# Weight splits on GpSimd cut into four pieces of 256 columns in most slots of a hybrid decoder step

## The chip, the cores and the metric

The kernel runs on one core of a Trainium2 chip. The metric is the time of one execution on the device in microseconds (us); the kernel before has a median of 2016.64 us over 3 runs (2014.04 to 2017.82).

## What is computed

One step of a one-layer decoder for two request groups that share all weights: a prompt of 1024 tokens and 8 samples of 4 tokens, together 1056 columns. The model width is 1024, everything is float32. Cut to what matters here:

```python
xn = rmsnorm(x, p["norm_mix_g"])
aq, ak, av, dq, dk, dvv, dz, da, db, ga, gb = split_cols(xn @ p["w_in"], IN_SPLITS)
ya = swa_prompt(aq, ak, av, p["sinks"])                     # window attention (sample: with cache)
qkv, new_dn_buf = causal_dwconv(jnp.concatenate([dq, dk, dvv], axis=-1), dn_buf, p["dn_conv_w"])
dq, dk, dvv = jnp.split(jax.nn.silu(qkv), 3, axis=-1)
o, new_S = gated_delta(qh, kh, heads(dvv), g, beta, dn_state, chunk)
yb = (rmsnorm(o, p["dn_norm_g"]) * jax.nn.silu(heads(dz))).reshape(B, L, DN_WIDTH)
mix = jax.nn.sigmoid(ga) * (ya @ p["w_br_a"]) + jax.nn.sigmoid(gb) * (yb @ p["w_br_b"])
h = x + mix @ p["w_mix_out"]
mk, mv = jnp.split(rmsnorm(mem, g) @ w_xkv, 2, axis=-1)     # memory keys and values
h = h + cross_attention(rmsnorm(h, p["norm_x_g"]) @ p["w_xq"], mk, mv) @ p["w_xo"]
u, gv = jnp.split(rmsnorm(h, p["norm_ffn_g"]) @ p["w_up"], 2, axis=-1)
u, new_ffn_buf = causal_dwconv(u, ffn_buf, p["ffn_conv_w"])
h = h + (jax.nn.silu(u) * gv) @ p["w_down"]
y = rmsnorm(h, final_norm_g)
```

The step also returns the new caches and states. It is one launch for both groups.

## The kernel before, in words

**A product in three.** A float32 matrix product is made of three products of numbers that are cut to fewer bits: weight W is split in a high part WH (W written in the type fp32r, with less of its mantissa) and a low part WL = W - WH, the activations x in XH and XL in the same way, and TensorE sums WH·XH + WH·XL + WL·XH into PSUM (`gemm_part`, line L542; `down`, L1969, has AH and AL in the place of XH and XL; `end_down`, L2001, has LASTH and LASTL; `gate_parts`, L1360). The 1056 columns go through in three chunks of 352. So one weight slot, of 128 rows by 1024 columns, is 8 blocks of 128 x 128 by 3 products by 3 chunks: 72 matmuls.

**Slots.** All weights lie in 136 slots of 512 KB, used in one order: attention 0 to 5, gate_a 6 to 9, the delta rule's q, k, v (dn) 10 to 21, gate_m 22 and 23, gate_b 24 to 29, dz 30 to 33, gate 34 to 37, branch 38 to 45, mix_kv 46 to 61, xq 62 to 65, xo 66 to 69, and the feed-forward stage 70 to 135, four in iteration 0 and six in each of iterations 1 to 10 (four for the up products of iteration f, then two for the `down` product of iteration f - 1; slots 132 and 133 are `down` of iteration 9). The last two, 134 and 135, are for `end_down`, which does the last `down` chunk by chunk with the final norm behind it. gate_m, gate_b and gate stand for tiles of the branch gates' product; those of slots 6 to 9 and 22 to 29 are early ones, stored in DRAM and loaded back later. In the delta stage, after the convolution of slots 22 and 23, `gate_parts` feeds small portions of these gate products into the gaps of the delta rule's chunks.

**Three engines per slot.** Slot n uses buffer p = n % 2 of RAW, WH and WL.
- SyncE's `loads` brings slot n's weights into RAW[p] once slot n-2 has been split (semaphore w_split). Its other transfers (gates, states, outputs) stand in the same queue.
- GpSimd's `split` waits for raw_in[p] (weights landed) and for w_used to reach n-1 (slots 0 to n-2 are used up, so the buffer is free). It writes WH = RAW * 1 (L755), adds 1 to w_hi, waits for w_hi, writes WL = RAW - WH (L757) and adds 1 to w_split. Its `one` is a constant of one column, broadcast over the free axis. Slot n is thus split while TensorE works on slot n-1.
- TensorE waits for w_split to reach n+1, runs the slot's matmuls, and adds 1 to w_used.

Slots 46 to 63 (HALVES) are split in two halves of 512 columns by `split_half` (L769 high, L771 low), the first half with semaphores of its own, so that a half can be split as soon as half a slot is used. All other slots are split whole, in two instructions. GpSimd has no other work, but for 19 adds of squares (L789, L792) for the final norm, which are behind the last split in its program.

**VectorE and ScalarE.** VectorE makes the low parts of the activations (L522 in `plain_rest`, L2452 in `split_rests`, L2617 in `rests`), the residual adds (L2597 in `mlp_down`), and the elementwise work between products. The places that the prediction goes through:
- Convolution of the delta rule's q, k, v (L2183 to L2209), with ScalarE's Silu (L929) behind it; small preparations of the next stage (L2401).
- Delta stage. `front` (L2273 to L2297) prepares a chunk of 128 tokens: t1, t2, t3 (L2276, L2278, L2280) make the decay masks, then a, q, k (L2284 to L2291) and v; `invert_quarters` (L2342 to L2361) inverts the chunk's triangular matrix by levels, alternating with TensorE (L1558): L2348 and L2355 are VectorE's steps, and each waits for TensorE's product before it and is waited for by the next one. `state` (L2371, L2373) multiplies the state by the decay and adds the chunk's update. All of this is one program order on VectorE.
- z multiply (L2447), after the delta stage.
- Branch products (L2459, L2463, L2465): for each tile t of 8, the gate times the accumulated product for both branches, and their sum. After t = 3 stand the seven adds of squares of the memory's norm (`norm_add`, L465), after t = 5 its eight scalings (`norm_dve`, L509) and eight low parts (L503), of 256 columns each; slot 45 is split during this.
- First norm of the feed-forward stage: L522 and L465 for eight tiles, then TensorE sums over partitions with a matrix of ones (`norm_sum`, L478).
- The last iteration of the feed-forward stage: `rests` (the two subtractions L2617) is put before `mlp_down` of the iteration before, and not behind it as in the others. While these run, TensorE begins slot 132 and GpSimd splits slot 133; TensorE's `down` waits for fd_free, which the residual adds L2597 raise. VectorE's line:

```python
if last:
    rests()
if not (isinstance(f, int) and f == 0):
    mlp_down(f - 1, FFN0(f) + 4)
if not last:
    rests()
```

**GpSimd's program order** around the change: `pairs(pool, 46, split)` (a loop over pairs of slots), the unrolled halves of 46 to 63, then a loop over pairs for 64 to 135, then the adds of squares.

Of the kernel before, what the change touches and what calls it, by code (L numbers as in the profile page):

```python
# [15 lines left out]
F32 = mybir.dt.float32  # L16
F32R = mybir.dt.float32r
ALU = mybir.AluOpType
# [21 lines left out]
SLOT = KT * P  # L40


SLOTS = {}
# [31 lines left out]


HALVES = SLOTS["mix_kv"][0], SLOTS["xq"][0] + 2
TURN = KT // 2
LEVEL_PARTS = (0, 3, 6, 8, 11, 14, 16, 20)
UNIT0 = 3 * (GA + GM)  # L80
# [60 lines left out]
def build(nc, d):  # L141
    ctx = ExitStack()
    with ctx:
        def sb(name, shape, dt=F32):
            return ctx.enter_context(nc.sbuf_tensor(name, shape, dt))

        def sem(name):
            return ctx.enter_context(nc.semaphore(name))

        def wait(eng, s, v):  # L150

            if not (isinstance(v, int) and v <= 0):
                eng.wait_ge(s, v)

        def pairs(eng, n, body):

            body(0, 0)
            body(1, 1)
            if n > 2:
                with eng.Fori(1, n // 2) as i:  # L160
                    body(2 * i, 0)
                    body(2 * i + 1, 1)
# [11 lines left out]
        RAW = sb("RAW", [P, 2, SLOT])  # L174
        WH = sb("WH", [P, 2, SLOT], F32R)
        WL = sb("WL", [P, 2, SLOT], F32R)
# [10 lines left out]
        def cst(name):  # L187
            a, n = CONST[name]
            return CST[:, a:a + n]
# [186 lines left out]
        def end_direct(c, m):  # L376

            return c == NCH - 1 and m >= KT - 2

        def end_add(c, m):  # L380
            return len([1 for x in END_UNITS[:END_UNITS.index((c, m)) + 1] if x[1] > 0 and not end_direct(*x)])
# [40 lines left out]
        raw_in = [sem("raw_in0"), sem("raw_in1")]  # L422
        w_hi, w_split, w_used = sem("w_hi"), sem("w_split"), sem("w_used")
# [17 lines left out]
        n = 0  # L441
# [5 lines left out]
        def norm_square(act, i, k, src, w):  # L447

            sq, ss, rs = norm_space(i)
            if k < 2:  # L450
                wait(act, nlo, 8 * i)
            else:
                act.wait_ge(nadd, 7 * i + max(1, k - 2))
            nc.scalar.activation(sq[:, k % 2, 0:w], src[:, k, :], ACT.Square).then_inc(nsq, 1)
# [60 lines left out]
        def plain_head(i, k, b, gain):  # L515

            nc.scalar.activation(XH[:, b, :], H[:, k, :], ACT.Copy, scale=gain[:, k:k + 1]).then_inc(nhi, 1)
# [8 lines left out]
        def gemm_tile(mm_g, p, k0, kn, off, xk0=0, ready=None, turn=0, between=None):  # L526

            for k in range(kn):
                if ready is not None:
                    nc.tensor.wait_ge(ready[0], ready[1] + xk0 + k + 1)  # L530
                mm = gemm_part(mm_g, p, k, kn, off, (k + turn) % KT - k if turn else xk0)
                if between is not None and k == between[1]:
                    between[0]()
            return mm
# [213 lines left out]
        @block.gpsimd  # L748
        def _(pool):
            one = cst("ones")[:, 0:1].to_broadcast([P, SLOT])  # L750

            def split(n, p, more=0):
                pool.wait_ge(raw_in[p], 8 * (n - p) + 16)
                wait(pool, w_used, n - 1)
                nc.gpsimd.tensor_tensor(WH[:, p, :], RAW[:, p, :], one, ALU.mult).then_inc(w_hi, 1)  # L755
                pool.wait_ge(w_hi, n + 1 + more)
                nc.gpsimd.tensor_tensor(WL[:, p, :], RAW[:, p, :], WH[:, p, :].bitcast(F32),  # L757
                                        ALU.subtract).then_inc(w_split, 1)
            pool.wait_ge(const_in, 16)
            def split_half(n, h):  # L760

                p, half = n % 2, slice(SLOT // 2 * h, SLOT // 2 * h + SLOT // 2)
                if h == 0:
                    pool.wait_ge(raw_in[p], 8 * (n - p) + 16)
                if h == 0 and n >= HALVES[0] + 2:
                    pool.wait_ge(w_half, n - HALVES[0] - 1)
                else:
                    pool.wait_ge(w_used, n - 1)
                nc.gpsimd.tensor_tensor(WH[:, p, half], RAW[:, p, half], one[:, 0:SLOT // 2], ALU.mult).then_inc(w_hi, 1)  # L769
                pool.wait_ge(w_hi, HALVES[0] + 2 * (n - HALVES[0]) + h + 1)  # L770
                nc.gpsimd.tensor_tensor(WL[:, p, half], RAW[:, p, half], WH[:, p, half].bitcast(F32),  # L771
                                        ALU.subtract).then_inc(w_split if h else w_first, 1)

            def rest_split(n, p):
                split(n, p, HALVES[1] - HALVES[0])
            pairs(pool, HALVES[0], split)
            for n in range(*HALVES):
                split_half(n, 0)
                split_half(n, 1)
            with pool.Fori(HALVES[1] // 2, NSLOTS // 2) as i:  # L780
                rest_split(2 * i, 0)
                rest_split(2 * i + 1, 1)

            for u, (c, m) in enumerate(END_UNITS):
                if m == 0 or end_direct(c, m):
                    continue
                pool.wait_ge(e_sqr, u + 1)
                if m == 1:
                    nc.gpsimd.tensor_tensor(e_ss[:, c, :], e_sq[:, (u - 1) % 6, :], e_sq[:, u % 6, :], ALU.add).then_inc(e_add, 1)  # L789
                else:  # L790
                    pool.wait_ge(e_add, end_add(c, m - 1))
                    nc.gpsimd.tensor_tensor(e_ss[:, c, :], e_ss[:, c, :], e_sq[:, u % 6, :], ALU.add).then_inc(e_add, 1)  # L792
# [3 lines left out]
        def _(act):  # L796
# [436 lines left out]
            for k in range(KT):  # L1233
                if k == KT - 1:
                    act.wait_ge(w_used, SLOTS["xo"][0] + 4)
                    for t in range(TURN, KT - 1):
                        plain_head(3, t, (t + TURN) % KT, cst("g_ffn"))
                act.wait_ge(xo_free, k + 1)
                if k < TURN or k == KT - 1:
                    plain_head(3, k, (k + TURN) % KT, cst("g_ffn"))  # L1240
                norm_square(act, 3, k, H, T)
# [51 lines left out]
        def _(pe):  # L1293
# [716 lines left out]
            def mlp_pe(f):  # L2010
                first = isinstance(f, int) and f == 0
                for j in range(4):
# [9 lines left out]
                    if first and j == 0:  # L2022
                        pe.wait_ge(xo_free, 7)
                    gemm_tile(j % 2, j % 2, 0, KT, 0, ready=(nlo, 24) if first and j == 0 else None, turn=TURN,
                              between=(lambda: norm_sum(pe, 3), KT - 2) if first and j == 0 else None).then_inc(w_used, 1)
# [9 lines left out]
        def _(dve):  # L2035
# [506 lines left out]
            for t in range(8):  # L2542
# [5 lines left out]
                if 2 <= t < 7:  # L2548
                    norm_add(dve, 3, t - 1, T)
                if 1 <= t <= TURN:  # L2550
                    plain_rest(dve, 3, t - 1, t - 1 + TURN, cst("g_ffn"))
# [209 lines left out]
```

## Time and profile before

| | before |
|---|---|
| runs, median (lowest to highest) | 2016.64 us (2014.04 to 2017.82) |
| profiled execution, own time | 2019.54 us |
| profiled execution, span of the trace | 2017.8 us |
| TensorE busy with matmuls | 1901.5 us, 94% |
| TensorE busy loading weights (beside matmuls) | 1789.3 us, 89% |
| VectorE busy | 1004.3 us, 50% |
| ScalarE busy | 489.3 us, 24% |
| GpSimd busy | 670.3 us, 33% |
| mean granted TensorE clock | 0.986 of full speed |
| chain that ended last, by engine | PE 68%, DVE 7%, ACT 3%, issue 2%, POOL 0% |

How to read it: the profile has one execution. Engines are named PE (TensorE's matmuls), PEld (TensorE's weight loads), DVE (VectorE), ACT (ScalarE), POOL (GpSimd) and SP (SyncE, which issues the transfers). PSUM accumulators are called PS, on-chip buffers by the program's names (WH, WL, RAW, H, YA, TMP, A, DV and so on; the name is that of the memory region, which several views share). "L757" is line 757 of the kernel. A row's busy time includes the time in which an instruction has begun and cannot go on. The chain that ended last follows the last instruction back to what released each step.

### The profile page before, as it was taken

What the parts mean: (1) busy time and instruction counts of PE and PEld (TensorE: products, weight loads), DVE (VectorE), ACT (ScalarE), POOL (GpSimd) and SP (SyncE); (2) the same over time, 40 slices, a digit from 0 to 9 for tenths busy, and PEclk for the clock granted to TensorE, in tenths of its full rate; (3) what the DMA queues carried; (4) which work ended last, traced back from release to release, by engine and by line L of the source; (5) the groups of instructions that cost most, each with busy time, mean ns of one, the idle gap of its engine ahead of it and who ended that gap; (6) DMA issues with size and microseconds to landing.
All of it is one profiled execution on the core that took longest, in us unless ns stands there. A gap on an engine that the chain in (4) does not pass through costs nothing.

```text
span 2017.8 us, 31812 instructions
## 1 busy us (share of the span) xinstructions
PE 1901.5 (94%) x13273; PEld 1789.3 (89%) x13273; DVE 1004.3 (50%) x1150; ACT 489.3 (24%) x908; POOL 670.3 (33%) x331
## 2 busy tenths in 40 slices
PE   6988999989989899999998799999999999999997
PEld 5966899977878788999988599999999999999997
DVE  6877267754453231564142437544454454345356
ACT  6055326632222103412031523100000000000012
POOL 3411033311100112545663024443343343343335
PEclk9999999999999999999999999999999999999999
DMA  4211111110102021422223111111111111111112
GB/s 184 90 38 43 34 43 42 39 57 25 34 26 64 28 93 51 149 85 95 74 84 122 67 36 43 51 42 52 42 42 45 48 42 48 45 42 45 48 46 86
DMA packets 45482, 119.71 MB, mean 59 GB/s; under 512 B 3808, under 2 KB 20896, under 8 KB 44224
## 3 DMA queue, kind: packets, MB, share of 16 engines
q1 hardware_dynamic: 45392, 118.39, 17.6%
q8 instruction: 71, 1.16, 0.2%
q14 instruction: 19, 0.16, 0.0%
HBM read 102.94 MB, written 15.77 MB: 59 GB/s over the span
## 4 chain that ended last, share of the span: by engine, by line
PE 68%; DVE 7%; ACT 3%; issue 2%; POOL 0%; DVEq 0%; ACTq 0%; POOLq 0%
PE PS L542 41%; PE PS L1969 11%; PE PS L1360 3%; PE PS L1558 2%; PE PS L1852 1%; PE PS L1596 1%; PE PS L1752 1%; ACT TMP L1205 1%; PE PS L1916 1%; DVE H L2632 1%; PE PS L1937 1%; PE PS L2001 1%; DVE XL L522 1%; PE PS L1643 0%; PE PS L1909 0%
## 5 line engine op out<-in xcount | busy, mean ns | idle before, releaser
L755 POOL TENSOR_TENSOR WH<-RAW,CST 128x1024 fp32r<-128x1024 f32 x118 | 238.9, 2025 | 1265.2 <-PE PS L542 678.6
L542 PE MATMUL PS<-XH,WH 128*128 128x352 f32 x2280 | 506.1, 330 | 34.4 <-POOL WL L757 13.4
L542 PE MATMUL PS<-XH,WL 128*128 128x352 f32 x2280 | 493.1, 324 | 0.0
L542 PE MATMUL PS<-XL,WH 128*128 128x352 f32 x2280 | 492.8, 324 | 0.0
L542 PEld LDWEIGHTS PS<-XH,WH 128*128 128x128 f32 x2280 | 389.5, 190 | 53.0 <-issue 35.8
L542 PEld LDWEIGHTS PS<-XH,WL 128*128 128x128 f32 x2280 | 392.9, 189 | 0.0
L542 PEld LDWEIGHTS PS<-XL,WH 128*128 128x128 f32 x2280 | 389.2, 189 | 0.0
L757 POOL TENSOR_TENSOR WL<-RAW,WH 128x1024 fp32r<-128x1024 f32 x118 | 317.8, 2693 | 9.3
L2597 DVE TENSOR_TENSOR H<-H,PS 128x1056 f32<-128x1056 f32 x80 | 100.2, 1254 | 130.3 <-PE PS L1969 130.3
L1267 ACT ACTIVATE AH<-TMP 128x1056 fp32r<-128x1056 f32 x20 | 20.8, 1082 | 353.6 <-PE PS L1969 341.1
L1969 PE MATMUL PS<-AH,WH 128*128 128x352 f32 x480 | 103.5, 324 | 1.9 <-DVE H L2597 1.9
L1969 PE MATMUL PS<-AL,WH 128*128 128x352 f32 x480 | 104.2, 325 | 0.0
L1969 PE MATMUL PS<-AH,WL 128*128 128x352 f32 x480 | 103.6, 324 | 0.0
L2610 DVE TENSOR_TENSOR TMP<-TMP,PS 128x1056 f32<-128x1056 f32 x22 | 27.6, 1254 | 151.8 <-PE PS L542 151.7
L1360 PE MATMUL PS<-XH,WH 128*128 128x352 f32 x240 | 87.8, 366 | 0.5
L1969 PEld LDWEIGHTS PS<-AH,WH 128*128 128x128 f32 x480 | 81.9, 188 | 2.2 <-DVE H L2597 2.2
L1969 PEld LDWEIGHTS PS<-AL,WH 128*128 128x128 f32 x480 | 81.9, 188 | 0.0
L1969 PEld LDWEIGHTS PS<-AH,WL 128*128 128x128 f32 x480 | 81.7, 188 | 0.0
L1360 PE MATMUL PS<-XH,WL 128*128 128x352 f32 x240 | 78.7, 328 | 0.0
L1360 PE MATMUL PS<-XL,WH 128*128 128x352 f32 x240 | 78.6, 328 | 0.0
L2573 DVE TENSOR_TENSOR TMP<-PS,TMP 128x1056 f32<-128x1056 f32 x22 | 27.6, 1257 | 92.6 <-PE PS L542 92.6
L1252 ACT ACTIVATE TMP<-TMP 128x32 f32<-128x32 f32 x22 | 5.1, 231 | 234.6 <-DVE TMP L2573 234.6
(460 smaller groups left out, 2524.2 us busy)
## 6 DMA issues: line engine op xcount, KB each, us to landing
RAW<-in_w SPq DMA_DIRECT2D x136, 512.0 KB, 3.5
H<-in_xT SPq DMA_DIRECT2D x4, 1056.0 KB, 9.0
TMP<-in_xT SPq DMA_DIRECT2D x2, 2112.0 KB, 8.6
early_gates<-DV SPq DMA_DIRECT2D x18, 176.0 KB, 2.0
out_yT<-H SPq DMA_DIRECT2D x4, 704.0 KB
early_gates<-A SPq DMA_DIRECT2D x12, 176.0 KB, 1.8
DV<-early_gates SPq DMA_DIRECT2D x1, 2112.0 KB, 14.0
TMP<-early_gates SPq DMA_DIRECT2D x2, 1056.0 KB, 5.5
```

The costliest lines, as they stand in the source:

```text
L522: nc.vector.scalar_tensor_tensor(XL[:, b, :], H[:, k, :], gain[:, k:k + 1], XH[:, b, :].bitcast(F32), ALU.mult, ALU.subtract).then_inc(nlo, 1)
L542: mm = nc.tensor.matmul(PS[:, 3 * mm_g + c, 0:CW], w_[:, p, off + k * P:off + (k + 1) * P], x_[:, xk0 + k, c * CW:(c + 1) * CW], start=fir ...
L755: nc.gpsimd.tensor_tensor(WH[:, p, :], RAW[:, p, :], one, ALU.mult).then_inc(w_hi, 1)
L757: nc.gpsimd.tensor_tensor(WL[:, p, :], RAW[:, p, :], WH[:, p, :].bitcast(F32), ALU.subtract).then_inc(w_split, 1)
L1205: nc.scalar.activation(x_s[:, p, h, :], x_ps(h, p), ACT.Exp, scale=xscale, bias=x_nm[:, p, 1, h:h + 1], accum_out=x_den[:, p, 0, h:h + 1]) ...
L1267: nc.scalar.activation((LASTH if last else AH)[:, i, :], f_act[:, i, :], ACT.Copy).then_inc(f_hi, 1)
L1360: mm = nc.tensor.matmul(PS[:, GATE_BANKS[g >= GA], 0:CW], w_[:, p, k * P:(k + 1) * P], x_[:, k, c * CW:(c + 1) * CW], start=(k == 0 and w_ ...
L1558: mm = nc.tensor.matmul(PS[out, bank + i, HP * j:HP * j + HP], lhs(h, r), rhs(h, r), start=True, stop=True)
L1969: mm = nc.tensor.matmul(PS[:, 3 * (m % 2) + c, 0:CW], w_[:, p, (m % 4) * 256 + k * P:(m % 4) * 256 + k * P + P], x_[:, k, bass.ts(c, CW)], ...
L2573: nc.vector.tensor_tensor(wide(x[:, 2:2 + T]), acc(i), wide(f_rs), ALU.mult).then_inc(fu_free, 1)
L2597: nc.vector.tensor_tensor(wide(H[:, m, :]), wide(H[:, m, :]), acc(m % 2), ALU.add).then_inc(fd_free, 1)
L2610: nc.vector.tensor_tensor(wide(f_act[:, i, :]), wide(f_act[:, i, :]), acc(i), ALU.mult).then_inc(f_gate, 1)
```

## The change

A new function `split_pieces` does what `split` does in four instructions of 256 columns for the high part, one wait for w_hi, and four of 256 columns for the low part. Only the last piece of each part adds 1 to its semaphore, so all counts stay the same, and TensorE still waits for the whole slot. It is used for slots 22 to 45 (from the memory-gate slots, gate_m, to the branch slots) and for slots 64 to 135 (the last two xq slots, xo, and the feed-forward stage). Slots 0 to 21 are still split whole, 46 to 63 in halves. No wait is put between the pieces of a part. Nothing changes on the other engines.

```diff
--- before.py
+++ after.py
@@ -75,6 +75,8 @@
 
 
 HALVES = SLOTS["mix_kv"][0], SLOTS["xq"][0] + 2
+FINE = SLOTS["gate_m"][0]
+PIECE = SLOT // 4
 TURN = KT // 2
 LEVEL_PARTS = (0, 3, 6, 8, 11, 14, 16, 20)
 UNIT0 = 3 * (GA + GM)
@@ -756,6 +758,19 @@
                 pool.wait_ge(w_hi, n + 1 + more)
                 nc.gpsimd.tensor_tensor(WL[:, p, :], RAW[:, p, :], WH[:, p, :].bitcast(F32),
                                         ALU.subtract).then_inc(w_split, 1)
+
+            def split_pieces(n, p, more=0):
+                pool.wait_ge(raw_in[p], 8 * (n - p) + 16)
+                wait(pool, w_used, n - 1)
+                cuts = [slice(c, c + PIECE) for c in range(0, SLOT, PIECE)]
+                for c in cuts[:-1]:
+                    nc.gpsimd.tensor_tensor(WH[:, p, c], RAW[:, p, c], one[:, 0:PIECE], ALU.mult)
+                nc.gpsimd.tensor_tensor(WH[:, p, cuts[-1]], RAW[:, p, cuts[-1]], one[:, 0:PIECE], ALU.mult).then_inc(w_hi, 1)
+                pool.wait_ge(w_hi, n + 1 + more)
+                for c in cuts[:-1]:
+                    nc.gpsimd.tensor_tensor(WL[:, p, c], RAW[:, p, c], WH[:, p, c].bitcast(F32), ALU.subtract)
+                nc.gpsimd.tensor_tensor(WL[:, p, cuts[-1]], RAW[:, p, cuts[-1]], WH[:, p, cuts[-1]].bitcast(F32),
+                                        ALU.subtract).then_inc(w_split, 1)
             pool.wait_ge(const_in, 16)
             def split_half(n, h):
 
@@ -772,8 +787,11 @@
                                         ALU.subtract).then_inc(w_split if h else w_first, 1)
 
             def rest_split(n, p):
-                split(n, p, HALVES[1] - HALVES[0])
-            pairs(pool, HALVES[0], split)
+                split_pieces(n, p, HALVES[1] - HALVES[0])
+            pairs(pool, FINE, split)
+            with pool.Fori(FINE // 2, HALVES[0] // 2) as i:
+                split_pieces(2 * i, 0)
+                split_pieces(2 * i + 1, 1)
             for n in range(*HALVES):
                 split_half(n, 0)
                 split_half(n, 1)
```

## Rows read from the trace of the kernel before

**Rows 1.** Stretches, feed-forward: us, PE, PEld, DVE, ACT, POOL, PEclk, DMA, GB/s.

```profile
1240.00:1952.00 712.00, 712.00 (x4399) 711.86 (x4398) 341.01 (x299) 61.26 (x115) 281.81 (x122) 1.00 0.14 45
```

**Rows 2.** Timeline, slot 26: start, us, engine, line, out<-in, count [idle <-releaser].

```profile
463.72 1.89 POOL L755 TENSOR_TENSOR WH<-RAW,CST 128x1024 fp32r<-128x1024 f32 x1 [35.77 <-PE PS L1360]
...
465.15 1.01 DVE L2278 TENSOR_TENSOR TMP<-TMP 128x512 f32<-128x512 f32 x1
465.69 2.70 POOL L757 TENSOR_TENSOR WL<-RAW,WH 128x1024 fp32r<-128x1024 f32 x1
466.19 2.75 DVE L2280 TENSOR_TENSOR TMP<-TMP 128x512 f32<-128x512 f32 x1
...
469.33 0.46 PE L1558 MATMUL PS<-TMP,A 64*64 64x64 f32 x16 [1.96 <-DVE TMP L2355]
...
470.91 0.69 DVE L2286 TENSOR_TENSOR TMP<-TMP 128x512 f32<-128x512 f32 x1
```

**Rows 3.** Timeline, the last split, slot 135.

```profile
1980.24 2.39 POOL L757 TENSOR_TENSOR WL<-RAW,WH 128x1024 fp32r<-128x1024 f32 x1
...
1982.68 0.59 PE L2001 MATMUL PS<-YAR,WH 128*128 128x352 f32 x2 [0.74 <-POOL WL L757]
```

**Rows 4.** Timeline of GpSimd, two halves without company.

```profile
939.34 1.29 POOL L771 TENSOR_TENSOR WL<-RAW,WH 128x512 fp32r<-128x512 f32 x1
...
940.59 1.04 POOL L769 TENSOR_TENSOR WH<-RAW,CST 128x512 fp32r<-128x512 f32 x1
```

**Rows 5.** Lines, shapes apart, GpSimd (busy us, mean ns | idle before).

```profile
L789 POOL TENSOR_TENSOR DV<-DV 128x352 f32<-128x352 f32 x3 | 2.8, 941 | 1.4 <-ACT DV L1286 1.4
```

**Rows 6.** Timeline, a half beside a run of VectorE.

```profile
1037.87 8.65 DVE L522 SCALAR_TENSOR_TENSOR XL<-H,CST,XH 128x1056 fp32r<-128x1056 f32 x4
...
1039.08 2.05 POOL L769 TENSOR_TENSOR WH<-RAW,CST 128x512 fp32r<-128x512 f32 x1
```

**Rows 7.** Timeline, slot 27's split.

```profile
502.79 1.89 POOL L755 TENSOR_TENSOR WH<-RAW,CST 128x1024 fp32r<-128x1024 f32 x1 [34.40 <-PE PS L1360]
...
503.44 1.79 DVE L2371 TENSOR_TENSOR TMP<-TMP 128x512 f32<-128x512 f32 x1
...
506.47 1.54 DVE L2290 TENSOR_TENSOR A<-H,A 128x512 f32<-128x512 f32 x1
```

**Rows 8.** Timeline of VectorE, end of the convolution.

```profile
408.75 0.27 DVE L2401 MEMSET TMP<- 64x256 f32 x1 [2.69 <-ACT DV L929]
```

**Rows 9.** Timeline, slot 133.

```profile
1952.75 1.89 POOL L755 TENSOR_TENSOR WH<-RAW,CST 128x1024 fp32r<-128x1024 f32 x1 [7.35 <-PE PS L542]
...
1953.81 5.32 DVE L2617 TENSOR_TENSOR YAR<-TMP,YAR 128x1056 fp32r<-128x1056 f32 x2
...
1960.34 0.75 PE L1969 MATMUL PS<-AH,WH 128*128 128x352 f32 x3 [1.92 <-DVE H L2597]
```

**Rows 10.** Timeline, slot 38's split behind a run of VectorE.

```profile
806.33 7.36 POOL L755 TENSOR_TENSOR WH<-RAW,CST 128x1024 fp32r<-128x1024 f32 x1 [9.16 <-PE PS L542]
...
807.18 4.75 DVE L2447 TENSOR_TENSOR H<-H,A 128x1056 f32<-128x1056 f32 x4
```

**Rows 11.** Timeline, slots 45 and 46, beside the memory's norm.

```profile
891.39 1.89 POOL L755 TENSOR_TENSOR WH<-RAW,CST 128x1024 fp32r<-128x1024 f32 x1 [5.41 <-PE PS L542]
...
892.57 1.83 DVE L2465 TENSOR_TENSOR DV<-DV,TMP 128x1056 f32<-128x1056 f32 x1
...
894.32 3.01 DVE L509 SCALAR_TENSOR_TENSOR YA<-H,CST,YA 128x256 f32<-128x256 f32 x2
...
903.05 1.04 POOL L769 TENSOR_TENSOR WH<-RAW,CST 128x512 fp32r<-128x512 f32 x1 [6.39 <-PE PS L542]
...
905.68 1.22 PE L542 MATMUL PS<-XH,WH 128*128 128x352 f32 x3 [2.78 <-DVE DV L2459]
```

**Rows 12.** Timeline, slot 71 and the feed-forward stage's norm.

```profile
1227.74 6.52 DVE L522 SCALAR_TENSOR_TENSOR XL<-H,CST,XH 128x1056 fp32r<-128x1056 f32 x3
...
1237.88 2.04 PE L478 MATMUL PS<-TMP,CST 128*128 128x352 f32 x6 [1.20 <-DVE TMP L465]
```

## Prediction, made before the change was run

> **What bounds the kernel now.** I read the busy time by stretches first. In the feed-forward stage TensorE works without a break: 712.00 us of 712 [rows 1]. Its 4399 matmuls at 72 to a slot are 61.1 slots, so a slot lasts 11.65 us there, and GpSimd's split of a slot has that long. Nothing done to the split can shorten this stretch, only its two ends. So the change is worth something only where TensorE stands idle and the engine it waits for had been kept waiting by a split. I looked for those places next, in order of time, with three engines side by side.
>
> Two views give the mechanism. In the delta stage VectorE's instruction at L2280, 128x512 with both inputs in SBUF, takes 2.75 us; one of the same shape, L2286, takes 0.69 a little later [rows 2]. The long one starts at 466.19, while GpSimd's low-part subtraction runs (465.69 to 468.39), and ends 0.55 after it. So it stood still until GpSimd's whole instruction was over, and what is queued behind it on VectorE is L2355, for which TensorE then idles 1.96 us. Instructions with one input in PSUM show no such wait.
>
> **The price of a piece.** Whole, the high part takes 1.89 [rows 2] and the low part 2.39 [rows 3]; halves of 512 take 1.04 and 1.29 [rows 4]. Half the columns save 0.85 and 1.10, so 256 columns should take 1.04 - 0.43 = 0.61 and 1.29 - 0.55 = 0.74. An add of 352 columns takes 0.94 [rows 5], where the low part's line gives 0.95. An instruction with no wait ahead of it starts 0.04 before its predecessor's end (939.34 + 1.29 against 940.59) [rows 4]. A split in pieces is then 4 x 0.61 + 4 x 0.74 - 6 x 0.04 + 0.08 (the wait for the high part, 465.69 less 463.72 + 1.89) = 5.24, against 1.89 + 0.08 + 2.39 = 4.36: 0.9 more. Bounds: 0 if the fixed part hides behind the piece before; 3.2 if a piece costs as much as 352 columns (8 x 0.94 = 7.5). I take 0.9, which two sizes and the add give.
>
> **Who gets in between pieces.** Where halves meet a run of VectorE's two-input instructions, a half takes 2.05 instead of 1.04, and four VectorE instructions of some 1.3 take 8.65 [rows 6]. A VectorE instruction that waited runs once the piece ends, the next GpSimd piece waits for that one, and VectorE's next waits for the piece: they take turns. So a lone VectorE instruction now waits at most one piece, 0.61 or 0.74, but a dense run pays a piece per instruction until the split is through.
>
> **Part by part**, times counted from the split's start: high pieces start at 0, 0.57, 1.14, 1.71, low ones from 2.40.
>
> *Delta stage.* Slot 26 starts at 463.72. L2278 wants the port at 465.15, in the third piece, and is through at 466.16 as before; the fourth piece ends at 466.77, L2280 at 467.46 instead of 468.94: 1.5 saved, below the 1.96 of idle. Slot 29 has the same pattern 123 us later: 1.5. Slot 27 starts at 502.79 [rows 7]. L2371 wants 503.44 and waits for the second piece to 503.97: it ends 0.57 sooner. L2290 then comes at 505.90, just as the first low piece starts (505.92): a wait of 0 to 0.74, 0.4 on the mean, so it ends at 507.0 and not 508.01: 1.0. Slot 30 repeats this: 1.0. Sum -5.0. Bounds: -3.5, if two pieces win each time, and -6, if none does in 27 and 30. In the other slots of this stage no VectorE wait is followed by an idle TensorE, so 0; if a piece hits one there, at most 0.74.
>
> *Slots 22 and 23*, the convolution. VectorE's run is dense; I put it at 4.1 of pieces instead of some 2.5 of waits per slot. After the last such run VectorE itself stands idle for 2.69, waiting for ScalarE's Silu [rows 8]: ScalarE is what is late there, and 1.6 more of VectorE fits. Cost 0; without that cover up to 1.6.
>
> *Slot 133's split*, end of the feed-forward stage. Both L2617 take from 1953.81 to 1959.13, the residual add behind them comes late, and TensorE idles 1.92 [rows 9]. In pieces the first starts at 1953.93 (end of the second piece) and ends at 1955.1 (a two-input instruction of 1056 takes 1.2, a quarter of 4.75 [rows 10]), the second waits for the third piece and ends at 1957.0. The add is done 2.1 sooner, 0.2 before TensorE asks: -1.9. If one more piece gets in: -1.3.
>
> *The last split.* TensorE already waits 0.74 for it [rows 3], so the longer split counts in full: +0.9 (0 to 3.2). GpSimd's 19 adds of squares queue behind it; they start as much later as TensorE's products do, so nothing more.
>
> *Slot 45*, last of the branch slots, under the memory's norm. VectorE's L2465 and the two L509 wait some 0.6 and 2.1 (1.83 less 1.2; 3.01 for two short ones) and fourteen more short instructions follow; at their end TensorE idles 2.78 [rows 11]. In turns with the pieces this run pays 0.57 + 0.58 for the last two high pieces and 4 x 0.74 = 4.1, not 2.7; I take +1.3. Then, being late, it meets slot 46's halves, which come at 903.05 whatever happens, with two or three instructions left where one was: up to two more halves, 1.04 and 1.3. So +1.3 to +3.6; I take the middle, 2.4.
> What a half does that arrives in a moving run is the open point. The high part that came at 806.33 took 7.36 instead of 1.89, since VectorE's run of L2447 went on to 811.9 [rows 10]: GpSimd had to wait for the run's end, which speaks for 1.3. But that run was already moving when GpSimd came, and ours will have been stopped before, hence the middle.
> The Trainium skill (SBUF — State Buffer, Who interferes with whom) says that whoever issues first gets the shared pair for the whole instruction and that issue order decides. By it GpSimd would have got in after one VectorE instruction at 806, which this trace contradicts; by the page slot 45 costs 3.6 and the sum below is -1.7, by that row 1.3 and -4.0.
>
> *Slot 71*, first norm of the feed-forward. TensorE idles 1.20 for the last L465, at the end of a dense run of six (three L522, then L465, L522, L465) whose first three take 6.52 where three of 1.2 would take 3.7 [rows 12]: 2.8 of waits. Six turns of 0.1, 0.61, 0.61 and three of 0.74 make 3.5: +0.7 (-1.2, when all that idle time goes, to +1.4, twice that).
>
> *The feed-forward slots between.* Per slot 5.24 plus three VectorE instructions of 1.3 in turn is 9.1, below 11.65: hidden. If that cover went, each of 61 slots would cost. SP's load of the slot after next is issued when the split ends, 0.9 later, with a whole slot in hand: 0.
>
> **Sum**: -5.0 - 1.9 + 0.9 + 2.4 + 0.7 = -2.9 us. The profiled execution took 2019.54 (span 2017.8), 0.14% above the median 2016.64; on the median that gives 2013.7.
>
> **Rivals.** (a) *VectorE keeps the port once it has it.* Then the run of slot 45 waits only for two pieces, 1.2 instead of 2.7, and ends before slot 46's halves come, which saves the 0.8 it waits there too: -2.3; slot 71 gives its 1.2. Sum -5.0 - 1.9 + 0.9 - 2.3 - 1.2 = -9.5: 2007.1. For it: 806.33 [rows 10]. Against: the turns at 1037 [rows 6].
> (b) *A piece has a dear fixed part*, and the result is slower. At 0.94 a piece the last split costs 3.2, slot 45 some 6 (eight dearer turns, three halves), slot 71 1.7, and the gains shrink to 3.4 and 1.9: +5.6, 2022.2. It tips from gain to loss at about 0.77 a piece on the mean, where I have 0.68. Against: 352 columns at 0.94, 512 at 1.04 and 1.29 lie on a line.
> (c) *The change doesn't do what it says*: with no wait between pieces GpSimd keeps the port from first to last. Then VectorE waits 2.3 and 2.9 instead of 1.9 and 2.4: delta +3.2, slot 133 +1.3, slot 45 +1.9, slot 71 and the tail +0.9 each: +8.2, 2024.8. Against: at 1039.08 a half started with no wait behind another, and VectorE got in [rows 6].
>
> **Chances.** This kernel's runs tell some 0.2%, 4.0 us, from no change. The forecast has 0.62 and its own range runs over that border: -5.5 to 0, 2011.1 to 2016.6; 0.22 of it lies beyond the border and 0.40 within. (a) has 0.22, all faster. (b) has 0.09: 0.07 slower, 0.02 within. (c) has 0.07, slower. Faster 0.44, within 0.42, slower 0.14. The range reaches from (a) to the forecast's upper end and the runs' scatter: 2007 to 2018.
>
> **What would show it.** In the changed profile: pieces of about 0.61 and 0.74, a split without company of 5.2; L2280 of slots 26 and 29 at 1.3 or less; TensorE's 1.92 beside slot 133's split gone; the wait for the last split at 1.6; TensorE's 2.78 at slot 45's end grown to 4 to 6. The forecast is wrong if that last one shrinks (a), if a lone piece takes over 0.8 (b), or if VectorE's waits reach from the first piece to the fourth (c).

## The result, and the profile after

The changed kernel takes 2004.03 us, median of 5 runs (1997.79 to 2005.60), against 2016.64 (2013.98 to 2018.90, 5 runs): a ratio of 0.9933 with a 95% interval of 0.9921 to 0.9946. That is 12.6 us faster, where 2.9 was forecast; 2004.03 lies 3 us below the range. The profiled execution has a span of 2002.1, 15.7 less than before, at a mean granted clock of 0.991 in place of 0.986.

The profile page, engines: VectorE is busy 46 us less, since its waits for the port count as busy, and GpSimd 162 us more.

```profile
PE 1891.3 (94%) x13273; PEld 1781.6 (89%) x13273; DVE 958.1 (48%) x1150; ACT 489.9 (24%) x908; POOL 832.1 (42%) x907
```

The timeline of slot 26's split, with the lines of [rows 2] in the changed kernel (line numbers are 18 higher there: L2296 and L2298 are L2278 and L2280). L767 and L768 are the high pieces, L771 and L772 the low ones.

```profile
462.88 1.75 POOL L767 TENSOR_TENSOR WH<-RAW,CST 128x256 fp32r<-128x256 f32 x3 [34.28 <-PE PS L1378]
...
464.31 0.87 DVE L2296 TENSOR_TENSOR TMP<-TMP 128x512 f32<-128x512 f32 x1
...
464.59 1.06 POOL L768 TENSOR_TENSOR WH<-RAW,CST 128x256 fp32r<-128x256 f32 x1
...
465.21 0.98 DVE L2298 TENSOR_TENSOR TMP<-TMP 128x512 f32<-128x512 f32 x1
...
466.58 0.32 PEld L1576 LDWEIGHTS PS<-TMP,A 64*64 64x64 f32 x16 [0.34 <-DVE TMP L2373]
```

L2298 takes 0.98 instead of 2.75. TensorE's matmul stream no longer stands still here, and its weight load waits 0.34. Three high pieces take 1.75 together, so 0.61 each with 0.04 of overlap, as worked out.

The other places that the prediction went through, in the changed kernel's timeline: slot 133 [rows 9], the last split [rows 3], the run of short instructions under slot 45 [rows 11], and slot 71 [rows 12].

```profile
1939.28 2.84 DVE L2635 TENSOR_TENSOR YAR<-TMP,YAR 128x1056 fp32r<-128x1056 f32 x2
...
1966.05 0.73 POOL L772 TENSOR_TENSOR WL<-RAW,WH 128x256 fp32r<-128x256 f32 x1
...
1966.83 0.58 PE L2019 MATMUL PS<-YAR,WH 128*128 128x352 f32 x2 [1.59 <-POOL WL L772]
...
880.06 1.69 DVE L2483 TENSOR_TENSOR DV<-DV,TMP 128x1056 f32<-128x1056 f32 x1
881.67 1.71 DVE L511 SCALAR_TENSOR_TENSOR YA<-H,CST,YA 128x256 f32<-128x256 f32 x2
883.30 0.95 DVE L505 TENSOR_TENSOR AL<-YA,AH 128x256 fp32r<-128x256 f32 x1
...
886.46 0.42 DVE L505 TENSOR_TENSOR AL<-YA,AH 128x256 fp32r<-128x256 f32 x1
...
889.89 0.99 DVE L505 TENSOR_TENSOR AL<-YA,AH 128x256 fp32r<-128x256 f32 x2
...
890.53 1.25 POOL L784 TENSOR_TENSOR WH<-RAW,CST 128x512 fp32r<-128x512 f32 x1 [4.79 <-PE PS L544]
...
892.19 0.72 PE L544 MATMUL PS<-XH,WH 128*128 128x352 f32 x3 [1.81 <-DVE DV L2477]
...
1213.11 5.07 DVE L524 SCALAR_TENSOR_TENSOR XL<-H,CST,XH 128x1056 fp32r<-128x1056 f32 x3
...
1223.35 2.04 PE L480 MATMUL PS<-TMP,CST 128*128 128x352 f32 x6 [1.30 <-DVE TMP L467]
```

Both L2635 take 2.84 instead of 5.32, and no row shows TensorE waiting behind the residual add of slot 133 any more. The wait for the last split is 1.59, where 1.6 was forecast. Under slot 45 TensorE waits 1.81 instead of 2.78, where a longer wait was forecast. At slot 71 it waits 1.30 instead of 1.20.

**Where the 15.7 us of the trace went.** The two programs have the same 13273 matmuls in the same order, so the shift of each is read by counting. It changes in steps: -2.05 at slot 26, -1.1 at 27, -2.1 at 29, -1.1 at 30, -1.0 at slot 45 for VectorE's run, +0.1 at slot 71, -2.1 at slot 133, +0.8 at the last split. These are waits, and they sum to -8.5. The rest, -7.3, comes where no wait differs: -1.7 and -2.6 in the stretches behind slots 27 and 30, -1.35 behind slot 36, -1.0 behind slot 45, -0.7 ahead of slot 10, where the programs are the same. There the matmuls themselves run faster, as far as the granted clock tells: the trace of before shows it lower in these places. Busy time by stretches behind slot 27, before and then after (columns: us, busy time and count of PE, PEld, DVE, ACT, POOL, granted clock, DMA share, GB/s):

```profile
507.60:515.60 8.00, 7.20 (x47) 6.25 (x49) 4.64 (x10) 1.10 (x3) 0.00 (x0) 0.59 0.20 68
```

```profile
503.00:511.00 8.00, 6.08 (x66) 5.14 (x66) 5.33 (x11) 1.50 (x5) 3.14 (x4) 1.00 0.21 68
```

Before, TensorE's clock is down to its lower level (1.2 of 2.4 GHz) for most of these 8 us, behind 2.0 us of idle time; after, behind 0.9 us of idle time, it stays up.

**How time and clock go together.** Each run lists its mean granted clock. One slope fitted over 163 runs of 14 kernels (60 runs of the kernel before; the change in two samples) says that time rises within a kernel by 15 us for each 0.01 of clock, and leaves 0.96 us of scatter, so runs can be compared at equal clock. That column of the table is read as the waits' part, and the rest of the gain as the clock's; the slope shows that the two move together, not what moves the clock. The ± is twice the standard error, worked out from the 0.96 and the numbers of runs; the change's two samples together give -7.7 ± 0.6.

| kernel | ratio (95% interval) | mean clock | us at equal clock |
|---|---|---|---|
| before | | 0.9878 | 0 |
| the change | 0.9933 (0.9921 to 0.9946) | 0.9912 | -8.0 ± 0.9 |
| the change, again (f0_change) | 0.9949 (0.9931 to 0.9966) | 0.9897 | -7.4 ± 0.8 |
| e1_delta | 0.9959 (0.9943 to 0.9975) | 0.9905 | -6.0 ± 0.8 |
| e2_s27_30 | 0.9981 (0.9971 to 0.9992) | 0.9902 | -1.5 ± 0.6 |
| e3_s26_29 | 0.9972 (0.9960 to 0.9984) | 0.9904 | -3.4 ± 0.6 |
| e4_rest | 0.9994 (0.9981 to 1.0007) | 0.9873 | -2.8 ± 0.6 |
| f1_last_whole | 0.9945 (0.9927 to 0.9963) | 0.9893 | -8.9 ± 0.8 |
| f2_halves | 0.9958 (0.9942 to 0.9974) | 0.9912 | -3.5 ± 0.8 |
| f3_eighths | 0.9979 (0.9967 to 0.9990) | 0.9888 | -1.6 ± 0.6 |
| g1_s45_whole | 0.9939 (0.9922 to 0.9956) | 0.9917 | -7.1 ± 0.8 |
| g2_gates_too | 0.9932 (0.9917 to 0.9947) | 0.9910 | -10.1 ± 0.8 |
| g3_where_it_pays | 0.9924 (0.9906 to 0.9942) | 0.9907 | -11.1 ± 0.8 |
| g4_halves_cut | 0.9915 (0.9899 to 0.9932) | 0.9902 | -14.5 ± 0.9 |
| i2_joined | 0.9893 (0.9877 to 0.9910) | 0.9905 | -15.1 ± 1.0 |

### The profile page after: what moved, and what is told of

Same layout as the page of the kernel before. It is cut to its first block, busy times and chain, and to the rows that moved or that the text cites. A ratio compares the mean times of both kernels' runs of the same rounds, so it can differ in the third digit from the quotient of the medians.

```text
span 2002.1 us, 32389 instructions
## 1 busy us (share of the span) xinstructions
PE 1891.3 (94%) x13273; PEld 1781.6 (89%) x13273; DVE 958.1 (48%) x1150; ACT 489.9 (24%) x908; POOL 832.1 (42%) x907
## 4 chain that ended last, share of the span: by engine, by line
PE 68%; DVE 7%; ACT 3%; issue 1%; POOL 0%; DVEq 0%; ACTq 0%; POOLq 0%
PE PS L544 42%; PE PS L1987 12%; PE PS L1378 3%; PE PS L1576 2%; PE PS L1870 1%; PE PS L1614 1%; PE PS L1770 1%; DVE XL L524 1%; ACT TMP L1223 1%; PE PS L1934 1%; DVE H L2650 1%; PE PS L1955 1%; PE PS L2019 1%; PE PS L1661 0%; PE PS L1927 0%
## 5 line engine op out<-in xcount | busy, mean ns | idle before, releaser
L767 POOL TENSOR_TENSOR WH<-RAW,CST 128x256 fp32r<-128x256 f32 x288 | 195.1, 705 | 827.4 <-PE PS L544 407.0
L544 PE MATMUL PS<-XL,WH 128*128 128x352 f32 x2280 | 492.4, 324 | 0.0
L771 POOL TENSOR_TENSOR WL<-RAW,WH 128x256 fp32r<-128x256 f32 x288 | 260.3, 931 | 7.5
L757 POOL TENSOR_TENSOR WH<-RAW,CST 128x1024 fp32r<-128x1024 f32 x22 | 45.2, 2055 | 265.2 <-PE PS L544 140.9
L768 POOL TENSOR_TENSOR WH<-RAW,CST 128x256 fp32r<-128x256 f32 x96 | 90.4, 941 | 0.0
## 6 DMA issues: line engine op xcount, KB each, us to landing
DV<-early_gates SPq DMA_DIRECT2D x1, 2112.0 KB, 14.2
```

Source lines behind the costliest of these rows:

```text
L544: mm = nc.tensor.matmul(PS[:, 3 * mm_g + c, 0:CW], w_[:, p, off + k * P:off + (k + 1) * P], x_[:, xk0 + k, c * CW:(c + 1) * CW], start=fir ...
L767: nc.gpsimd.tensor_tensor(WH[:, p, c], RAW[:, p, c], one[:, 0:PIECE], ALU.mult)
L768: nc.gpsimd.tensor_tensor(WH[:, p, cuts[-1]], RAW[:, p, cuts[-1]], one[:, 0:PIECE], ALU.mult).then_inc(w_hi, 1)
L771: nc.gpsimd.tensor_tensor(WL[:, p, c], RAW[:, p, c], WH[:, p, c].bitcast(F32), ALU.subtract)
```

## The experiments

### One part of the change alone: e1 to e4

Each keeps `split_pieces` for the named slots and gives the others back to `split`. The edit of the first (slots 22 to 31) and of the second (27 and 30):

```diff
-            with pool.Fori(FINE // 2, HALVES[0] // 2) as i:
+            with pool.Fori(FINE // 2, 16) as i:
                 split_pieces(2 * i, 0)
                 split_pieces(2 * i + 1, 1)
+            with pool.Fori(16, HALVES[0] // 2) as i:
+                split(2 * i, 0)
+                split(2 * i + 1, 1)
...
-            pairs(pool, FINE, split)
+            pairs(pool, 26, split)
+            for n in range(26, 32):
+                (split_pieces if n in (27, 30) else split)(n, n % 2)
```

> Pieces in slots 22 to 31 alone (convolution and delta stage), all other slots as before the change. Waits-and-clock theory: the changed kernel's trace lost 2.05, 1.1, 2.1 and 1.1 us of TensorE's idle time in slots 26, 27, 29 and 30, and behind 27 and 30 also two stretches of 6.8 us at half the granted clock that followed idle times of 2.0 us before; together -6.4 - 1.7 - 2.7 = -10.8 us, and no half-clock stretch behind slots 27 and 30. Chance theory: the half-clock stretches come and go between executions whatever the splits do, so only the waits count: -6.4 us, and half-clock stretches behind 27 and 30 in some traces. The prediction on record had -5.0 for this part.

> Pieces in slots 27 and 30 alone. Waits-and-clock theory: -1.1 each of idle time, and -1.7 and -2.7 from the two half-clock stretches that no longer follow: -6.6 us, and after both slots TensorE's granted clock stays at 1.00. Chance theory: -2.2 us, half-clock stretches as likely as before.

> Pieces in slots 26 and 29 alone, whose idle time of 2 us was not followed by a half-clock stretch in the trace before. Both theories: -2.05 and -2.1, so -4.2 us; the half-clock stretches behind slots 27 and 30 stay by the waits-and-clock theory (granted clock 0.57 there). If the gain is near -8, the clock answers to something else than those idle times.

> Pieces in slots 32 to 45 and 64 to 135, whole in 22 to 31: the complement of the first run. Read from the changed kernel's trace: slot 45 -1.0 for VectorE's shorter run (plus up to 1.0 from the clock behind it), slot 133 -2.1, last split +0.8, slot 71 +0.1: -2.2 to -3.2 us. By the terms of the prediction on record (slot 45 +2.4, slot 71 +0.7) it would be +2.1. If the two parts don't add up to the whole change's -12.6, something joins them.

Measured, medians against the 2015.79 of before: 2006.44, 2011.19, 2008.36 and 2014.70, so -9.4, -4.6, -7.4 and -1.1. The delta stage carries the change: e1 alone gives three quarters of it. At equal clock the waits are -6.0, -1.5, -3.4 and -2.8; the traces gave -6.4, -2.2, -4.2 and -2.2 to -3.2, so the first three fall 0.4 to 0.8 short and the last fits. And e1 and e4 together (-8.8 ± 1.0) are close to the whole change.

With the terms of the prediction e4 would have come out slower; it did not.

The chance theory of the clock fails as stated: four kernels with pieces in the delta stage (e1, e2, e3 and the change itself) have a mean clock of 0.990 to 0.991, e4 without them 0.987, near the 0.988 of before. But the waits-and-clock theory fails too, at e3. There slots 27 and 30 are whole, and TensorE idles behind them as long as before. The groups of TensorE's matmuls by line from 480 to 660 us, before and then in e3 (busy us, mean ns | idle before them <-releaser), and third the busy time of the stretch behind slot 27 in e3:

```profile
L1584 PE MATMUL PS<-TMP 64*64 64x64 f32 x24 | 2.0, 224 | 4.0 <-DVE TMP L2355 4.0
```

```profile
L1604 PE MATMUL PS<-TMP 64*64 64x64 f32 x24 | 2.0, 224 | 4.1 <-DVE TMP L2375 4.0
```

```profile
502.00:510.00 8.00, 5.81 (x65) 5.15 (x65) 4.97 (x10) 1.86 (x5) 0.28 (x1) 1.00 0.21 68
```

Two idle times of 2.0 us each, as before, and the clock stays at 1.00 behind slot 27.

### More traces for the clock: j1 and j2

The kernel before and e3, unchanged, one more execution each.

> One more trace of the kernel before, to see whether the two stretches at half clock behind slots 27 and 30 are there in every execution. Theory that the 2.0 us of idle time there brings the clock down each time: granted clock near 0.57 behind both again. Theory that such an idle time brings it down in some executions only: 1.00 behind one or both, or half-clock stretches in other places.

> One more trace of the kernel with pieces in slots 26 and 29 alone; its first trace had no half-clock stretch behind slots 27 and 30 although TensorE idled 2.0 us there as before. Theory that the idle time there brings the clock down each time, which the first trace speaks against: 0.57 this time. Theory that it does so in some executions only, where it falls in the chip's own time: either. If the clock stays at 1.00 again, the idle times of slots 26 and 29 may have had a part in it.

The kernel before fell to half clock behind both slots again (first row, 0.57 behind slot 27), as e4 had (0.58); e3's kernel stayed up again (second row).

```profile
506.50:514.50 8.00, 7.33 (x46) 6.38 (x48) 4.51 (x10) 1.10 (x3) 0.00 (x0) 0.57 0.20 68
```

```profile
504.50:512.50 8.00, 5.87 (x65) 5.15 (x65) 4.90 (x10) 1.93 (x5) 0.21 (x1) 1.00 0.24 68
```

So the length of the idle time alone doesn't decide, and pure chance is unlikely: in three executions of three (before, e4, j1) the 2.0 us brought the clock down, and in two of two with pieces in slots 26 and 29 it did not. There the work ahead was 2 us shorter, so the idle time behind slot 27 came sooner: it ended at 503.22 and 505.65 us, against 507.17 to 508.40 in the three.

e2 shows the reverse at slot 29, which is whole there. Its 2.02 us of idle time in the timeline, and the busy time of the 4 us that follow (columns as above), in the kernel before and then in e2:

```profile
592.28 0.46 PE L1558 MATMUL PS<-TMP,A 64*64 64x64 f32 x16 [2.02 <-DVE TMP L2355]
592.00:596.00 4.00, 3.72 (x65) 3.27 (x65) 2.30 (x5) 0.94 (x2) 0.00 (x0) 1.00 0.43 131
```

```profile
588.09 0.46 PE L1578 MATMUL PS<-TMP,A 64*64 64x64 f32 x16 [2.02 <-DVE TMP L2375]
588.00:592.00 4.00, 3.91 (x61) 3.50 (x62) 2.17 (x5) 0.75 (x2) 0.00 (x0) 0.70 0.43 131
```

The same idle time, 4 us sooner, brings the lower level for a part of the 4 us in e2, and none in the kernel before. This speaks for the moment at which the idle time falls. But the kernels differ in other idle times too (e3 has next to none at slots 26 and 29), and a kernel that only shifts the work was not made, so the cause is not shown.

### The size of a piece: f0 to f3

```diff
-PIECE = SLOT // 4
+PIECE = SLOT // 2
...
-            with pool.Fori(HALVES[1] // 2, NSLOTS // 2) as i:
+            with pool.Fori(HALVES[1] // 2, NSLOTS // 2 - 1) as i:
                 rest_split(2 * i, 0)
                 rest_split(2 * i + 1, 1)
+            rest_split(NSLOTS - 2, 0)
+            split(NSLOTS - 1, 1, HALVES[1] - HALVES[0])
```

The first hunk is f2 (f3 has 8 in the place of 2), the second f1.

> The change itself, beside the three sizes below. So far time fits waits + 1485 us x (1 - mean granted clock) over 76 runs, with 0.95 us of scatter. Two-part theory: -7.9 us at equal clock and about -4.4 us because TensorE's granted clock is higher on the mean (0.991 against 0.988). Chance theory of the clock: -7.9 at equal clock again, but the clock part of another sample lies near 0, so the median gains some 8 us, not 12.

> The change with slot 135, the last one, split whole again. The trace of the change has the first matmul behind the last split 0.76 us later against the one before it: -0.8 us against the change at equal clock, TensorE's wait for the last split back at 0.74 us. If the time is the same, the longer last split was hidden by something behind it.

> The change with pieces of 512 columns in place of 256. Waits theory (a VectorE instruction waits for the piece that is running, at most 1.04 or 1.29 us): by the times in the trace before, slots 26, 29, 27 and 30 give some -0.8 each, slot 133 -1.5, slot 45 -0.5, the last split +0.3: -4.9 us at equal clock against the kernel before, so 3.0 us worse than the change. Rival, that any cut is enough since it is the wait over both parts that hurts: -7.9 as with four pieces, or better by the shorter last split.

> The change with pieces of 128 columns. From 1.89 and 1.04 us (and 2.39 and 1.29) a piece of 128 should take 0.40 and 0.46, a split without company 6.4 us, and the last split costs 2.0 us more than whole, 1.2 more than with four pieces. The waits left in slots 27 and 30 shrink by some 0.4 each: -7.5 us at equal clock against the kernel before, 0.4 worse than the change. If a piece has a floor (0.6 or more), a split takes 9 us and the result is some 5 us worse than the change.

f0: -7.4 at equal clock, 0.9897 of clock: the clock part was -2.8 in this sample and -5.1 in the first, so it is there in both and not steady. f1: TensorE's wait for the last split is 0.75 again, and at equal clock it is 1.2 ± 1.0 better than the change's two samples; the 0.8 of the trace fits. f2: -3.5, so halves give less than half of what quarters give, and less than the -4.9 expected. The rival, that any cut is enough, is out. f3: -1.6, far from the -7.5 expected, although a piece shows no floor: seven of 128 columns take 2.54 without company, 0.36 each. Its timeline early in the feed-forward stage shows what was missed:

```profile
1238.93 4.42 POOL L767 TENSOR_TENSOR WH<-RAW,CST 128x128 fp32r<-128x128 f32 x7 [3.01 <-PE PS L544]
...
1243.78 8.96 POOL L771 TENSOR_TENSOR WL<-RAW,WH 128x128 fp32r<-128x128 f32 x7
...
1246.90 5.54 DVE L2623 TENSOR_TENSOR H<-H,TMP 128x1056 f32<-128x1056 f32 x4
...
1252.71 0.45 POOL L772 TENSOR_TENSOR WL<-RAW,WH 128x128 fp32r<-128x128 f32 x1
1253.12 2.54 POOL L767 TENSOR_TENSOR WH<-RAW,CST 128x128 fp32r<-128x128 f32 x7
...
1253.21 0.75 PE L544 MATMUL PS<-XH,WH 128*128 128x352 f32 x3 [2.77 <-POOL WL L772]
```

Seven low pieces take 8.96 because GpSimd waits for a VectorE instruction ahead of six of them (8.96 by 7 is 1.28). The split then takes 14.2 (1238.93 to 1253.16), no longer fits into its slot's 11.65 us, and TensorE waits 2.77 for it. This is one place of several: matmul by matmul against the change, TensorE also idles 2.7 longer at 812 us among the branch slots (3.80 for 1.14), 2.4 longer behind the convolution (2.93 for 0.50) and 1.1 longer at the last split. Turns cost the side with the small pieces.

### Slot 45, the early gates, and the halves: g1 to g4

```diff
+            with pool.Fori(FINE // 2, HALVES[0] // 2 - 1) as i:
...
+            split(HALVES[0] - 2, 0)
+            split(HALVES[0] - 1, 1)
...
-                nc.gpsimd.tensor_tensor(WH[:, p, half], RAW[:, p, half], one[:, 0:SLOT // 2], ALU.mult).then_inc(w_hi, 1)
+                q0, q1 = slice(half.start, half.start + PIECE), slice(half.start + PIECE, half.stop)
+                nc.gpsimd.tensor_tensor(WH[:, p, q0], RAW[:, p, q0], one[:, 0:PIECE], ALU.mult)
+                nc.gpsimd.tensor_tensor(WH[:, p, q1], RAW[:, p, q1], one[:, 0:PIECE], ALU.mult).then_inc(w_hi, 1)
```

The first hunk is g1; the second, in `split_half` and with the same done to the low part, is g4. g2 puts a loop of `split_pieces` over slots 6 to 11 into the part that is whole; g3 has `split` in all slots that its text doesn't name. g2, g3 and g4 leave the last slot whole, as f1 does.

> The change with slots 44 and 45 split whole again. The prediction on record made pieces in slot 45 a loss of 2.4 us (so whole: 2.4 us better than the change, -10.2 us at equal clock against the kernel before). The changed kernel's trace shows a gain: VectorE's run from L2465 to L2459 took 10.74 us in place of 11.72, so whole again: 1.0 us worse than the change at equal clock (-6.8), TensorE's idle time before slot 45's matmuls back from 1.8 to 2.8 us.

> The change with the last slot whole, and with pieces in slots 6 to 11 too (early gates beside the window attention). In slots 8, 9 and 10 of the kernel before, L2092, which has 4 columns, takes 1.99 us because it waits 1.82 for the whole low part, and TensorE idles 1.1 us behind its chain each time. Turns theory: L2092 and L2094 now wait for a piece each at most (0 to 0.74 each), so 0.4 to 1.1 of each 1.1 is saved: -1.2 to -3.3 us against the run with the last slot whole, at equal clock -10 to -12 against the kernel before. Rival, that a chain of short two-input instructions pays a piece per instruction: 0 or a loss of some 1 us.

> Pieces only where TensorE was seen to wait behind a split (slots 6 to 11, 24 to 31, 44 and 45, 132 and 133), whole elsewhere but for the halves. If pieces in all other slots are hidden, this is as the run before it: within 0.5 us at equal clock. If they cost something that is spread thinly (GpSimd's longer splits, VectorE's turns), it is faster by over 0.5.

> The change with the last slot whole, and with the halves of slots 46 to 63 cut in two pieces of 256 columns. There VectorE's runs are dense (L2452 and L522 of 1056 columns, each waiting 0.8 to 1.1 for a half). Turns theory: a dense run pays for all of GpSimd's pieces whatever their size, and two pieces of 0.61 cost 0.2 more than a half of 1.04: no gain, 0 to 1.5 us slower than the run with the last slot whole. Rival, that smaller pieces always help VectorE: 1 to 2 us faster, since TensorE idles 1.9 and 2.8 us beside slots 47 to 49.

g1: TensorE's wait ahead of slot 45's matmuls is 2.78 again, to the hundredth that of [rows 11]. At equal clock it is 0.6 ± 1.0 slower than the change's two samples, and not 2.4 faster: pieces in slot 45 are no loss.

g2: -10.1 against the -8.9 of f1, at the low end of what was expected. L2118, which is L2092, takes 0.17 in slot 8 instead of 1.99; the chain behind it then meets the low pieces, and TensorE's wait shrinks from 1.14 to 0.30 (the kernel before, then g2):

```profile
133.99 2.36 POOL L757 TENSOR_TENSOR WL<-RAW,WH 128x1024 fp32r<-128x1024 f32 x1
134.38 1.99 DVE L2092 TENSOR_TENSOR TMP<-TMP,CST 128x4 f32<-128x4 f32 x1
...
135.27 0.17 DVE L2118 TENSOR_TENSOR TMP<-TMP,CST 128x4 f32<-128x4 f32 x1
135.30 2.11 POOL L771 TENSOR_TENSOR WL<-RAW,WH 128x256 fp32r<-128x256 f32 x3
```

Slots 9 and 10 give as much (1.1 and 0.8). At 107 us the rival has its say: two instructions of this chain pay for a piece each there (0.60 and 0.65), and TensorE waits 2.61 where it waits 1.95 in f1.

g3: 1.0 ± 1.1 better than g2, so whether pieces in the hidden slots cost anything is not told.

g4: -14.5, 5.6 ± 1.2 better than f1, and here the expectation was wrong in sign. The timelines of f1 and then of g4 in the norm ahead of the memory attention, where VectorE's run is dense:

```profile
1022.33 8.66 DVE L524 SCALAR_TENSOR_TENSOR XL<-H,CST,XH 128x1056 fp32r<-128x1056 f32 x4
1023.53 2.06 POOL L784 TENSOR_TENSOR WH<-RAW,CST 128x512 fp32r<-128x512 f32 x1
...
1025.67 2.19 POOL L786 TENSOR_TENSOR WL<-RAW,WH 128x512 fp32r<-128x512 f32 x1
...
1029.03 0.75 PE L544 MATMUL PS<-XH,WH 128*128 128x352 f32 x3 [0.54 <-DVE XL L524]
```

```profile
1018.86 6.32 DVE L524 SCALAR_TENSOR_TENSOR XL<-H,CST,XH 128x1056 fp32r<-128x1056 f32 x4
...
1020.73 1.74 POOL L789 TENSOR_TENSOR WL<-RAW,WH 128x256 fp32r<-128x256 f32 x1
...
1022.43 1.63 POOL L785 TENSOR_TENSOR WH<-RAW,CST 128x256 fp32r<-128x256 f32 x1
1022.53 0.75 PE L544 MATMUL PS<-XH,WH 128*128 128x352 f32 x3 [2.12 <-POOL WL L789]
...
1025.10 1.67 DVE L467 TENSOR_TENSOR YA<-YA 128x1056 f32<-128x1056 f32 x1
```

The engines take strict turns in both. Four VectorE instructions take 8.66 beside halves, as in [rows 6], and 6.32 beside quarters, in which the first had no wait. Quarters stay in the run longer, and here TensorE first waits 2.12 for the low part, where f1 waits 0.97 for XL; behind that f1 waits four more times for XL, 2.86 in all, and g4 once, 0.36. In sum 2.48 against 3.83. More was won where the low parts behind the branch products are made (L2472 in f1, L2475 in g4; f1, then g4):

```profile
910.37 7.79 DVE L2472 TENSOR_TENSOR XL<-DV,XH 128x1056 fp32r<-128x1056 f32 x4
910.50 0.75 PE L544 MATMUL PS<-XH,WH 128*128 128x352 f32 x3 [1.37 <-DVE XL L2472]
...
908.32 6.67 DVE L2475 TENSOR_TENSOR XL<-DV,XH 128x1056 fp32r<-128x1056 f32 x4
908.46 0.75 PE L544 MATMUL PS<-XH,WH 128*128 128x352 f32 x3
```

There f1 waits 1.37, 0.55, 0.30 and 0.53 for one XL tile after the other, and g4 not at all: GpSimd has time, so what counts is VectorE's pace, not the sum of the pieces. The expectation had summed them. The two places make 4.1 of the 5.6 ± 1.2.

### Joined: i2

> The parts that paid, joined: pieces of 256 in slots 6 to 11, 24 to 31, 44 and 45, 132 and 133, the halves of slots 46 to 63 cut in two pieces, whole elsewhere. At equal clock against the kernel before: pieces only where they pay gave -11.1, and the cut halves gave 5.6 more than the same kernel without them (-14.5 against -8.9). If the parts add up: -16.7 at equal clock, with the clock part some 1999 us. If the cut halves owe their gain to what the other slots' pieces set up, it stays near -14.5 or less.

1996.53 us against 2018.25 in the same job, 0.9893 (0.9877 to 0.9910): the fastest kernel of the study by its median, and ahead of the change. At equal clock -15.1 ± 1.0: 4.1 ± 1.2 beyond g3, so the cut halves keep most of their gain without the pieces elsewhere, and the parts don't quite add up to 16.7. From g4, with pieces in the other slots too, it is not told apart at equal clock (0.6 ± 1.3).

## Why the prediction was wrong

The side was right and the size was not: the chance of faster by over 0.2% had 0.44, and 0.6% came. With the -7.7 of equal clock alone the time would be 2008.9, inside the range; the clock took it out. Two things failed, a term of the sum and something that the sum did not have.

**The price of a piece** held: 0.61 and 0.73 measured, 0.61 and 0.74 worked out, a split without company takes 5.2 (1949.82 to 1955.05 us in the changed kernel), and the last split's wait came out at 1.59.

**The price of a turn** was the step that failed ("a dense run pays a piece per instruction"). A VectorE instruction that takes turns loses the piece less some 0.2, not the whole piece. In g4 a VectorE instruction of 1.25 takes 1.67 beside a high piece (0.42 lost for one of 0.61) and 1.79 beside a low one (0.54 for 0.73). [rows 6] had it in sight: an L522 without company takes 1.31, so the four that take 8.65 lose some 3.4, where the halves that they meet, by [rows 4], are two of 1.29 and two of 1.04, 4.7 in all. With this price slot 45 has no extra delay: after L2483, five short instructions lose 2.3, and with its own 0.4 the run loses 2.7, as much as it lost to the whole split. It was put at 4.1, or at 1.3 more on the whole. Being no later, the run's last instruction had begun when slot 46's half came (890.53), which spared it the 0.8 that it waits there before. So +2.4 is -1.0, on rival (a)'s side in this slot, though not by its mechanism: VectorE did not keep the port, the turns were cheap. g1 rules the forecast loss out.

The same price made slots 26 and 29 -2.1 each, not -1.5: L2298 lost 0.3 to its piece, not 0.6, and the 1.96 went whole. And it made slot 71 +0.1, not +0.7. Slots 27 and 30 (-1.1 for -1.0), slot 133 (-2.1 for -1.9) and the last split (+0.8 for +0.9) stood. The corrected sum is -8.5, of which the runs at equal clock show -7.7 ± 0.6. Rival (a)'s -9.5 lies near too, and its sign, a shorter wait at slot 45, came true, but by luck: at slot 45 it had -2.3 for -1.0 and at slot 71 -1.2 for +0.1, and the turns in f1 and g4 contradict its mechanism.

**Left out: TensorE's clock.** The profile of before had it in sight: its granted clock was 0.986, and 0.59 behind slot 27, where the prediction had counted idle time only. The mean clock rose to 0.9904 over 11 runs of the change, which is worth 3.9 us by the slope, and it rose in every kernel that had pieces in the delta stage. No rival had that. Why the clock stayed up is open: it goes with when an idle time falls (e3, j2, e2), but that was not tried by itself. That it moves from run to run by as much (the kernel before went from 2012 to 2023 us in one job) is why the change's two samples differ by 2.8 us in their means.

**The rule of the Trainium skill** that was weighed (SBUF — State Buffer, Who interferes with whom: the engine that issues first has the pair for the whole instruction) is what the turns in f1 and g4 show, instruction by instruction. The cost that the page would have given slot 45 (3.6) did not come. GpSimd's high part of slot 38, which waited through a whole run of VectorE before [rows 10], did so again in pieces; the first of three, merged here, took most of the time:

```profile
793.76 7.23 POOL L767 TENSOR_TENSOR WH<-RAW,CST 128x256 fp32r<-128x256 f32 x3 [8.30 <-PE PS L544]
794.61 4.76 DVE L2465 TENSOR_TENSOR H<-H,A 128x1056 f32<-128x1056 f32 x4
```

That doesn't fit the rule as the prediction read it. Why a run that is already moving is not broken into there, and is in slots 62 and 63, stays open.

Rivals (b) and (c) are out: no piece without company took over 0.75, and no VectorE wait reached over the pieces.

## What to carry to other kernels

When two engines take turns at a port, cut the work of the one with slack small enough that the other keeps pace with the engine that feeds on it, and no smaller: eighths lost most of what quarters won, because the split then missed its own slot. Cut where the idle time of the bounding engine follows from the wait; pieces elsewhere won nothing, and whether they cost anything was not told. Leave the last split, which nothing covers, whole. And read the granted clock beside each idle time: here some third of the gain came with a higher clock, and runs compared at equal clock told 1 us apart where medians moved by 3.

## What was not expected of the hardware

- TensorE's granted clock fell to half for 6.8 us behind an idle time of 2.0 us, in three executions of three; the same idle time, with 2 us less work ahead of it, did not bring it down in two of two. Another of 2.02 us was followed by a fall in e2 and by none in three traces where it came 3 to 4 us later.
- VectorE instructions as small as 128x4 wait for the whole of a GpSimd instruction: L2092 took 1.99 us in slot 8 of the kernel before, and 0.17 with pieces.
- Run to run, the time of a kernel follows its mean granted clock with 0.96 us of scatter, over a range of 11 us.
